# Memory heads taken in pairs, in four steps of their own in a finer order, and the weights' exponential ahead of softplus

## The reference, cut to what matters

```python
def memory_branch(q_mem, mem, norm_mem, w_mem_kv):
    k_m, v_m = jnp.split(rmsnorm(mem, norm_mem) @ w_mem_kv, 2, axis=-1)
    q, k, v = _heads(q_mem, N_MEM_HEADS), _heads(k_m, N_MEM_HEADS), _heads(v_m, N_MEM_HEADS)
    sc = jnp.einsum('bqhd,bkhd->bhqk', q, k).astype(jnp.float32) * HEAD_DIM ** -0.5
    p = jax.nn.softmax(sc, axis=-1)
    o = jnp.einsum('bhqk,bkhd->bqhd', p.astype(v.dtype), v)
    return o.reshape(q_mem.shape)
...
# first layer, stick-breaking attention, for each of 12 heads
log_stay = jnp.where(causal, -jax.nn.softplus(z), 0.0)
later = lax.cumsum(log_stay, axis=3, reverse=True) - log_stay
w = jnp.where(causal, jnp.exp(jax.nn.log_sigmoid(z) + later), 0.0)
```

## Time and profile before

| | |
|---|---|
| median of three runs | 1241.72 us (1241.18 to 1242.05) |
| profiled execution, its own time | 1241.92 us |
| span in the profile | 1239.7 us, so 2.2 us lie around it |
| PE (TensorE) busy | 1209.7 us, 98% of the span |
| weight loads (PEld) | 998.0 us, 81% |
| DVE, ACT, POOL busy | 801.3, 554.7, 103.9 us |
| granted TensorE clock, mean | 0.999 of full |
| first layer's memory heads | 66.0 to about 106 us |
| second layer's memory heads | 675 to about 715 us |

### The profile page before, as it was taken

One profiled execution on the slowest core, in us unless ns is written; L12 is line 12 of the kernel. 1 busy time (PEld: TensorE's weight loads), 2 busy tenths in 40 slices (PEclk: granted clock), 3 DMA queues, 4 the chain that ended last, 5 costly groups with the idle time before them and its releaser, 6 DMA issues.

```text
span 1239.7 us, 17005 instructions
## 1 busy us (share of the span) xinstructions
PE 1209.7 (98%) x5975; PEld 998.0 (81%) x5975; DVE 801.3 (65%) x1251; ACT 554.7 (45%) x918; POOL 103.9 (8%) x133
## 2 busy tenths in 40 slices
PE   5999999999999999999999999999999999999997
PEld 5877888887888888878887888788788888878886
DVE  5775666767777777752257776876777777774226
ACT  5555666645444444431144553535444444442122
POOL 0301433423000000000011000001100000000000
PEclk9999999999999999999999999999999999999999
DMA  7412111113233333323241222222233333333551
GB/s 241 136 56 65 52 52 52 52 58 97 85 102 102 90 96 101 90 96 102 91 147 35 65 73 68 65 63 78 86 102 95 92 102 102 92 111 104 127 140 71
DMA packets 176388, 112.50 MB, mean 91 GB/s; under 512 B 20110, under 2 KB 168014, under 8 KB 176334
## 3 DMA queue, kind: packets, MB, share of 16 engines
q1 hardware_dynamic: 175936, 111.62, 30.2%
q10 hardware_dynamic: 398, 0.16, 0.1%
HBM read 107.58 MB, written 2.10 MB: 88 GB/s over the span
## 4 chain that ended last, share of the span: by engine, by line
PE 88%; DVE 6%; ACT 2%; issue 2%; POOL 1%; DMA 1%; ACTq 0%; DVEq 0%; POOLq 0%
PE bank L1416 18%; PE bank L1418 17%; PE bank L1417 17%; PE bank L1739 8%; PE bank L1712 8%; PE bank L1725 2%; PE bank L1752 2%; PE bank L1660 1%; DVE w_lo L930 1%; PE bank L1584 1%; PE bank L1586 1%; PE bank L1585 1%; PE bank L1608 1%; PE bank L1610 1%; PE bank L1609 1%
## 5 line engine op out<-in xcount | busy, mean ns | idle before, releaser
L1416 PE MATMUL bank<-y_hi,w_hi 128*128 128x512 f32 x928 | 365.1, 393 | 1.7 <-DVEq L1078 1.0
L1418 PE MATMUL bank<-y_hi,w_lo 128*128 128x512 f32 x928 | 361.7, 390 | 0.0
L1417 PE MATMUL bank<-y_lo,w_hi 128*128 128x512 f32 x928 | 361.4, 389 | 0.0
L930 DVE TENSOR_TENSOR w_lo<-raw,w_hi 128x1024 fp32r<-128x1024 f32 x188 | 230.6, 1226 | 166.8 <-ACT w_hi L585 162.8
L585 ACT ACTIVATE w_hi<-raw 128x1024 fp32r<-128x1024 f32 x186 | 196.4, 1056 | 285.3 <-PE bank L1418 137.1
L1416 PEld LDWEIGHTS bank<-y_hi,w_hi 128*128 128x128 f32 x928 | 174.2, 188 | 39.7 <-issue 3.0
L1418 PEld LDWEIGHTS bank<-y_hi,w_lo 128*128 128x128 f32 x928 | 174.2, 188 | 36.9
L1417 PEld LDWEIGHTS bank<-y_lo,w_hi 128*128 128x128 f32 x928 | 174.3, 188 | 36.1 <-issue 1.0
L1712 PE MATMUL bank<-ar,w_hi 128*128 (+1 forms) x288 | 88.7, 390 | 0.8 <-DVE af L1173 0.8
L787 ACT ACTIVATE af<-af,conv 128x512 f32<-128x512 f32 x88 | 63.1, 717 | 38.2 <-DVE af L1173 38.1
L1739 PE MATMUL bank<-w_hi,ar 128*128 128x512 f32 x288 | 77.1, 390 | 0.8 <-DVE af L1173 0.8
(11 more groups left out here) (205 smaller groups left out, 1612.8 us busy)
## 6 DMA issues: line engine op xcount, KB each, us to landing
raw<-in_a_ffn_up SPq DMA_DIRECT2D x44, 512.0 KB, 3.8
raw<-in_b_ffn_up SPq DMA_DIRECT2D x44, 512.0 KB, 3.8
raw<-in_a_ffn_down SPq DMA_DIRECT2D x22, 512.0 KB, 3.2
raw<-in_b_ffn_down SPq DMA_DIRECT2D x22, 512.0 KB, 3.7
raw<-in_a_w_in SPq DMA_DIRECT2D x20, 512.0 KB, 3.8
raw<-in_w_kv_shared SPq DMA_DIRECT2D x12, 512.0 KB, 3.9
raw<-in_a_w_out SPq DMA_DIRECT2D x8, 512.0 KB, 3.4
raw<-in_b_w_in SPq DMA_DIRECT2D x8, 512.0 KB, 3.8
```

The costliest lines, as they stand in the source:

```text
L930: nc.vector.tensor_tensor(w_lo[:, m % SPLIT, :], raw[:, m % RAW, :], w_hi[:, m % SPLIT, :].bitcast(F32), ALU.subtract).then_inc(lo_done, 1)
L1416: mm(bank, w[0], y[0][:, k, :], start=(k == 0), stop=False)
L1417: mm(bank, w[0], y[1][:, k, :], start=False, stop=False)
L1418: last = mm(bank, w[1], y[0][:, k, :], start=False, stop=(k == KT - 1))
```

## The change

Four things change.

1. A memory unit is no longer a head but a pair of heads and half of the queries (`f, hf = divmod(i % MH, 2)`); there are still four per layer. Its scores are 12 matmuls of 256 columns as before, but they alternate between rows 0 to 63 and rows 64 to 127 and between two banks. Its values are 12 matmuls of 256 columns with 128 columns of weights, where before they were 6 of 512 columns with 64 columns of weights: V of a pair is stored with 64 columns of zeros between the two heads (`vm_heads`, `vm_gaps`, as the attention's own V has it), so both heads add up in one bank of 128 partitions. POOL writes the zeros with two memsets at its start. The first unit waits for the first tile of memory queries alone, not for both.
2. `mem_slot` is gone. Its steps stand in the orders by themselves: C (scores, maximum, exponential), N (the scalings, DVE only), B (transposes and their copies), D (values and their copies).
3. Both orders are written anew: `SEQ_A` takes the place of `PRE` and `MEM_FILL` (F is a range of projection steps; 37 of them stand in this stage, before 38), and `SEQ_B` has the new letters and other places for S, V, G, R, W, T, A and a few P.
4. In the attention's slot, ACT makes the exponential of unit t-4 (now L761) ahead of the softplus pieces of unit t-1 (now L770 to L772).

Line numbers of the changed kernel are a few higher: its steps are L1420 to L1422, memory scores L1525, transposes L1535, values L1550.

```diff
-        bm = sb("bm", [P, 2048], F32R)
+        bm = sb("bm", [P, 2560], F32R)
...
-        vm = [t[:, 1024:2048].rearrange("p (s k f) -> p s k f", s=2, k=2) for t in (am, bm)]
+        vm = [t[:, 1024:2560].rearrange("p (s k f x) -> p s k f x", s=2, k=2, f=2) for t in (am, bm)]
+        vm_gaps = [t[:, 1024:2560].rearrange("p (n x d) -> p n x d", n=8, x=3)[:, :, 1, :] for t in (am, bm)]
...
-        PRE = 5
-        MEM_FILL = [(5, 12), (12, 19), (19, 26), (26, 33), (33, 38), None]
-        LEFT, SPREAD = 24 * PAIRS - 38, UP * (PAIRS - 1)
-        ATT_FILL = [(38 + LEFT * t // SPREAD, 38 + LEFT * (t + 1) // SPREAD) if t < SPREAD else None for t in range(U + 5)]
+        SEQ_A = [("F", 0, 3), ("C", 0), ("F", 3, 7), ("N", 0), ("F", 7, 11), ("B", 0), ("F", 11, 12), ("C", 1),
+                 ("F", 12, 15), ("N", 1), ("F", 15, 18), ("D", 0), ("F", 18, 19), ("B", 1), ("C", 2), ("F", 19, 23),
+                 ("N", 2), ("F", 23, 25), ("D", 1), ("F", 25, 26), ("B", 2), ("C", 3), ("N", 3), ("F", 26, 31),
+                 ("V", 0), ("F", 31, 32), ("D", 2), ("B", 3), ("F", 32, 37), ("D", 3)]
+        DONE = max(t[2] for t in SEQ_A if t[0] == "F")
+        LEFT, SPREAD = 24 * PAIRS - DONE, UP * (PAIRS - 1)
...
+        SEQ_B = [("P", 0, 0, 0, 3), ("C", 4), ("P", 0, 0, 3, 5), ("N", 4), ("P", 0, 0, 5, 8), ("P", 0, 1, 0, 5),
+                 ("B", 4), ("C", 5), ("P", 0, 1, 5, 6), ("N", 5), ("P", 0, 1, 6, 8), ("P", 0, 2, 0, 1), ("D", 4),
...
+            for gap in vm_gaps:
+                nc.gpsimd.memset(gap.bitcast(F32), 0.0).then_inc(vm_zero, 1)
...
+                if 4 <= t < U + 4:
+
+                    u = t - 4
+                    n = unit(u)[3]
+                    act.wait_ge(cum_done, u + 1)
+                    if u >= 2:
+                        act.wait_ge(wt_lo, u - 1)
+                    nc.scalar.activation(wf[:, u % 2, 0:n], ZB[u % 5][:, 0:n], ACT.Exp).then_inc(w_exp, 1)
                 if 1 <= t <= U:
...
+            def mem_max(i):
+                dve.wait_ge(ms_done, i + 1)
+                for b in range(2):
+                    ins = nc.vector.tensor_reduce(st[:, 8 + 2 * b:10 + 2 * b], banks[2 + b][:].rearrange("p (q k) -> p q k", q=2),
+                                                  AX_X, ALU.max, negate=True)
+                ins.then_inc(mmx, 1)
+
+            def mem_scale(i):
+                dve.wait_ge(mexp, 4 * (i + 1))
+                link(nc.vector.reciprocal(st[:, 16:20], st[:, 12:16]))
+                for qt in range(TT):
+                    ins = nc.vector.tensor_scalar(pm[:, M * qt:M * (qt + 1)], pm[:, M * qt:M * (qt + 1)],
+                                                  st[:, 16 + qt:17 + qt], None, ALU.mult)
+                ins.then_inc(mpn, 1)
 
...
+            def mem_scores(i):
+                l = i // MH
+                f, hf = divmod(i % MH, 2)
+                pe.wait_ge(kq_lo, (1, 15)[l] + f)
...
-                for qt in range(TT):
-                    o = banks[2 + qt // 2][:, M * (qt % 2):M * (qt % 2) + M]
+                for qt in range(2):
+                    q = slice(P * (2 * hf + qt), P * (2 * hf + qt + 1))
                     for s, (a, b) in enumerate(((0, 0), (0, 1), (1, 0))):
-                        last = mm(o, qms[i // MH][r:r + DH, a, f, P * qt:P * (qt + 1)], km[r:r + DH, b, f, :],
-                                  start=(s == 0), stop=(s == 2))
+                        for hp in range(2):
+                            r = slice(DH * hp, DH * (hp + 1))
+                            last = mm(banks[2 + hp][:, M * qt:M * (qt + 1)], qms[l][r, a, f, q], km[l][r, b, f, :],
+                                      start=(s == 0), stop=(s == 2))
                 last.then_inc(ms_done, 1)
 
...
-                    for s, (a, b) in enumerate(((0, 0), (0, 1), (1, 0))):
-                        last = mm(OB[0:DH, :], vm[:, a, kt, DH * m:DH * (m + 1)], pmTs[i // MH][:, b, kt, :],
-                                  start=(kt == 0 and s == 0), stop=(kt == 1 and s == 2))
+                    for hp in range(2):
+                        for s, (a, b) in enumerate(((0, 0), (0, 1), (1, 0))):
+                            last = mm(OB[:, half_queries(hf)], vm[l][:, a, kt, f, DH * hp:DH * hp + P],
+                                      pmTs[l][:, b, kt, M * hp:M * (hp + 1)],
+                                      start=(kt == 0 and hp == 0 and s == 0), stop=(kt == 1 and hp == 1 and s == 2))
                 last.then_inc(mav, 1)
...
-            fill((0, PRE))
-            for g in range(6):
-                mem_slot(0, g, 2)
-                for j in v_due(MEM_FILL, g):
-                    v_transpose(4 + j, TT)
-                fill(MEM_FILL[g])
+            for op, *a in SEQ_A:
+                if op != "N":
+                    {"C": mem_scores, "B": mem_transposes, "D": mem_values, "V": lambda j: v_transpose(4 + j, TT),
```

More of the change, by code:

```diff
@@ L659, in mem_v_high @@
                 l, f = divmod(iv, 2)
[L660 removed]
+                v_high(iv, vm_heads(l, 0, f), by_head(TR[:, 0:M].rearrange("p (k f) -> p k f", k=2)))
             for n in range(8):
@@ new lines, in mem_o_low, with mem_pt_low @@
+            def mem_o_low(i):
+                f, hf = divmod(i % MH, 2)
+                dve.wait_ge(mo_hi, i + 1)
+                nc.vector.tensor_tensor(oT_lo[:, 6 + f, half_queries(hf)], OB[:, half_queries(hf)],
+                                        oT_hi[:, 6 + f, half_queries(hf)].bitcast(F32), ALU.subtract).then_inc(mo_ev, 1)
+            def mem_pt_low(i):
+                pmT_l = pmTs[i // MH]
+                for kt in range(2):
+                    dve.wait_ge(mpt_hi, 2 * i + kt + 1)
+                    nc.vector.tensor_tensor(pmT_l[:, 1, kt, :], banks[4 + kt][:], pmT_l[:, 0, kt, :].bitcast(F32),
+                                            ALU.subtract).then_inc(mpt_lo, 1)
```

111 lines of the change are left out of this document (31 added, 80 removed), and 54 rows, old and new, of the table SEQ_B.

## The result

The changed kernel takes 1232.80 us (median of six runs, 1232.53 to 1233.61), the kernel before 1241.74 (six runs). The ratio is 0.9929, with an interval of 0.9919 to 0.9939: 8.9 us faster. The prediction was 1235.4, with a range of 1233.4 to 1238.4.

What follows compares the result with a forecast made beforehand. The prediction took PE's nearly gapless stream of matmuls to bound the kernel. From 1241.92 us, -5.5 + 0.8 + 0.7 - 2.6 + 0.3 = -6.3 gave 1235.6, less 0.2 for the median: 1235.4, range 1233.4 to 1238.4.

Steps and rivals of the forecast that it cites:

- scores, eight units: Memory scores: alternating row halves run side by side, 0.94 us a unit instead of 1.63; 5.5 us gained.
- values: Memory values: twelve matmuls of 256 columns take 1.48 us instead of 1.38 for six of 512; +0.8 us over eight units.
- seams: Projection steps following other work on PE: 19 such places instead of 12; +0.7 us, bounds 0 and 0.9.
- (a): First memory scores: the first unit no longer waits for the second query tile; -0.4 us.
- (b): First layer's memory stage: PE's wait for the V tile's low part on DVE goes; -1.1 us.
- (c): First attention: PE's two waits for the weights' exponential go, as ACT makes it first; -0.5 us.
- (d): Second layer, behind the fourth pair's scores: scalings ahead of scores shorten PE's wait, -0.5 us; a later low-part wait, 0.1 more.
- new waits of the memory units: Memory units' transposes waiting for DVE's scalings, and other handovers: +0.3 us in all, bounds 0 and 4.
- handovers: Allowance of +0.3 us for PE waiting on DVE in memory units; margins of 0.2 to 0.7 us at six of eight.
- rival on weight loads: Memory scores: twelve 128-column weight loads bound a unit, which stays at 1.63 us; 1240.9 us in all, chance 0.05.
- seven more at 0.1: Seven added places where a step follows other work, each priced at 0.1 us; +0.7 us.

Runs made afterwards that it cites:

- e1: Changed kernel with memory scores in turns of six matmuls per head in the first layer and three in the second; 1234.49 us.
- e11: Changed kernel with memory scores in turns of 4, 4, 2, 2 matmuls in the first layer and 5, 5, 1, 1 in the second; 1233.82 us.
- e8: Changed kernel with one projection step of the tile behind the first V transpose moved ahead of the third unit's values; 1234.77 us.
- e12: Changed kernel, but each layer's first memory unit waits for both tiles of memory queries, as in the kernel before; 1237.75 us.
- e3: Changed kernel's pair units and early exponential, with the order and places of the kernel before in both layers; 1237.84 us.
- e14: Kernel before with only ACT's exponential of unit t-4 moved ahead of the softplus pieces of unit t-1; 1240.89 us.
- e10: Changed kernel with the second layer's fourth pair of scores ahead of the values of units 2 and 3; 1234.53 us.
- e5: Changed kernel with the transposes of the first layer's four memory units one projection step earlier each; 1233.50 us.
- e9: Changed kernel with the second layer's first two transposes of weights one projection step later; 1232.36 us.
- e7: Changed kernel with four second-layer moves by one step: first weight transposes, fifth weight transpose and last scores later, fifth V transpose earlier; 1232.38 us.

## Why the prediction was partly wrong, point by point

| term of the sum | forecast | measured |
|---|---|---|
| scores, eight units | -5.5 | -5.7 |
| values | +0.8 | +0.4 |
| seams | +0.7 | 0.0 |
| (a) second query tile | -0.4 | -0.4 |
| (b) V's low part | -1.1 | -1.1 |
| (c) exponential | -0.5 | -0.8 |
| (d) behind the fourth scores | -0.6 | -0.5 |
| new waits of the memory units | +0.3 | 0.0 |
| first transposes of weights | none | +0.2 |
| small seams and waits of that stretch | none | -0.2 |
| fifth V transpose a step earlier | none | -0.4 |
| sum | -6.3 | -8.5 |

The mechanisms were right. What failed is the size of terms of the sum, nearly all to the same side: first the step that prices the seams at +0.7 us where the runs show 0.0, then the values, priced 0.4 too high, the handovers, 0.3 too high, a wait put at nothing that brought 0.4, and the exponential, 0.3 too low.

- **Scores** right: eight groups of 0.90 to 0.91 us against 1.62. The rival on weight loads fell. The argument for the side-by-side run was sound; that it needs neighbours in the stream, which I took from the earlier trace rows, was not (e1, e11). Where the prediction gives twelve loads 1.28 us and says that the scores would gain nothing to speak of, its own numbers (1.63 - 1.28) leave a gain of 0.35 us a unit, 2.8 in all. At that price the rival would have lain nearer to the forecast than its 1240.9.
- **Seams**, the largest miss (0.7 us), is the step "seven more at 0.1". I priced the step behind short matmuls by the one behind scores, and counted only what is added. Values hand over for 0.02 us. Where the new order puts a step between transposes and scores, the dearer seam goes: the transposes take 0.79 instead of 0.96, which pays for the 0.09 behind them and the 0.10 ahead of the scores that come instead. In both memory stages the differences of the first table are those of scores, values and waits, with nothing left over (-2.86 + 0.21 - 0.42 - 1.14 = -4.21 against -4.19; -2.85 + 0.21 = -2.64 against -2.65).
- **Values** (0.4): the group of 24 matmuls of 256 columns has a seam of its own in its 2.96 us. I scaled it and added seams again. 1.43 is 12 x 0.12.
- **(a) and (b)** right in size, and (b) in cause (e8). (a) is the wait that e12 brings back, there 1.8 us long. But e3 shows that the sum's independent terms hide how they hang together: had the places stayed, the shorter scores would have made (b) twice as long, with the clock halved behind it in some executions, and a unit's transposes would have waited 0.9 us for scalings. By (b) and (d) I gave the new places 1.7 us; they are worth 5, of which some 3 are losses that the new units would bring without them.
- **(c)**: 0.8 and not 0.5. I took the total of the two waits that name L767; e14 shows 0.26 us more behind step 192, at a V transpose that waits for DVE, where I had looked for none.
- **(d)** right, and ended by the scores' last DVE row as forecast, as far as the times tell. The row names no releaser, but e10, which moves only these scores ahead, takes the wait away.
- **Handovers** (0.3): no memory unit waits. The measured margins of the transposes are 0.2, 0.9, 0.6 and 0.4 us in the first layer and 1.6, 0.7, 0.6 and 0.6 in the second: six of eight lie in the 0.2 to 0.7 that I had added up, and e5 shows the first to be real. The allowance was not needed.
- **Missing**: the fifth V transpose (0.4). I read the order of S, W and T there and not V's. Also missing, and offset by small things behind it that I don't take apart, is the longer wait of the first transposes of weights, which e9 shortens by 0.7 us.
- **The range** failed since I let bounds of terms offset each other. Seams, values and handovers all at their lower bound give 1233.6, and the two gains that I had too small (c) or not at all (the fifth V transpose) take 0.7 more: 1232.9, where the kernel lies.

## What to carry to other kernels

A stream that becomes shorter on one engine moves every handover: list what was hidden by a narrow margin first, since without new places this change kept 3.8 of 8.9 us (e3). Price a seam by the pair of groups that meet there, in both directions, and don't add it to a group's cost that holds one already. When a wait is moved, look at the next wait of the same engine: of five moves made here to gain more (four in e7, one in e10), one kept its whole gain.

## What the runs showed of the hardware

Matmuls of the upper and the lower 64 rows run side by side even where three or four of one half stand together: 0.90, 0.91, 0.92, 1.14 and 1.25 us for twelve with turns of 1, 3, 4, 5 and 6. All five fit one rule, made after the runs: the half that comes second starts once no more than three of the other are still to start.

TensorE's clock fell from 2.4 to 1.2 GHz behind 1.71 us (e12, twice) and 1.84 us (e3) of idle time, for some 3 us, and cost 1.5 to 1.7 us on top of the wait. It stayed at full behind 1.61 us (e8) and behind 1.87 us (e10, profiled execution). So a hole of that length can cost double, in some executions and not in others: the executions of e12 have a mean granted clock of 0.998 or 0.999 where they took 1236.1 to 1236.3 us, and of 0.996 where they took 1239.8 to 1240.2.
